# A fp32 encoder trunk on TensorE: another order of products at both ends of each MLP, ScalarE's squares, and smaller first loads

## What is computed

```python
for i in range(DEPTH):                      # 2 layers, x is (1, 512, 1024) float32
    h = rmsnorm(x, norm_mix_g[i])
    x = x + (pool_mixer(h, ...) if i == 0 else sgu_mixer(h, ...))
    h = rmsnorm(x, norm_mem_g[i]); m = rmsnorm(mem, norm_memkv_g[i])   # 256 memory tokens
    x = x + mem_attention(h, m, w_q, w_kv, w_o)                        # 4 heads
    h = rmsnorm(x, norm_ffn_g[i])
    x = x + jnp.square(jax.nn.relu(h @ w1)) @ w2                       # 1024 -> 4096 -> 1024
return rmsnorm(x, final_norm_g)
```

## Time and profile before

| what | value |
|---|---|
| median of 3 runs | 1170.44 us (1170.16 to 1172.05) |
| the profiled execution | 1171.35 us, its span 1169.3 us |
| TensorE (PE) busy | 1140.8 us, 98% of the span |
| VectorE (DVE) | 829.2 us, 71% |
| ScalarE (ACT) | 635.7 us, 54% |
| GpSimd (POOL) | 251.3 us, 21% |
| mean granted TensorE clock | 0.993 of full |
| chain that ended last, by engine | PE 82%, DVE 9%, DMA 3%, ACT 3%, issue 2% |

### The profile page before, as it was taken

The page is one execution under the profiler, slowest core; times in us unless marked ns, Lnnn a source line. Parts: engine busy times, 40 slices in busy tenths (PEclk is TensorE's granted clock), DMA queues, the critical chain, the costliest instruction groups (busy, mean ns, idle before and its releaser), DMA issues.

```text
span 1169.3 us, 16188 instructions
## 1 busy us (share of the span) xinstructions
PE 1140.8 (98%) x6556; PEld 1003.9 (86%) x6556; DVE 829.2 (71%) x933; ACT 635.7 (54%) x773; POOL 251.3 (21%) x211
## 2 busy tenths in 40 slices
PE   8999999999999999999999999999989999999997
PEld 6888888989999999788888888888989999999975
DVE  7787647677786786777487656655757678677778
ACT  7664434765555655545444432543576656556555
POOL 0040035113012121113164044004511211112020
PEclk9999999999999999999999999999999999999999
DMA  9523134969789777735232622313587977977673
GB/s 349 206 80 101 55 135 107 244 133 192 196 181 201 186 143 164 174 73 198 91 97 84 216 91 72 108 36 144 118 227 158 198 191 179 207 171 154 146 133 102
DMA packets 48457, 176.59 MB, mean 151 GB/s; under 512 B 5504, under 2 KB 5632, under 8 KB 47744
## 3 DMA queue, kind: packets, MB, share of 16 engines
q0 software_dynamic: 18432, 67.12, 31.9%
q1 hardware_dynamic: 28368, 104.35, 26.5%
q10 hardware_dynamic: 1584, 4.10, 1.0%
HBM read 173.45 MB, written 2.10 MB: 150 GB/s over the span
## 4 chain that ended last, share of the span: by engine, by line
PE 82%; DVE 9%; DMA 3%; ACT 3%; issue 2%; POOL 0%; SPq 0%; DVEq 0%; ACTq 0%; POOLq 0%
PE psum L1874 11%; PE psum L1876 11%; PE psum L1875 11%; PE psum L2149 8%; PE psum L2150 8%; PE psum L2151 8%; PE psum L2129 8%; PE psum L2131 7%; PE psum L2130 7%; DVE w_lo L1181 2%; DMA w_raw<-in_up 2%; DMA w_raw<-in_weights 1%; DVE w_lo L1170 1%; PE psum L2066 1%; ACT w_hi L725 1%
## 5 line engine op out<-in xcount | busy, mean ns | idle before, releaser
L1181 DVE TENSOR_TENSOR w_lo<-w_sum,w_hi 128x1024 fp32r<-128x1024 f32 x112 | 136.5, 1223 | 84.2 <-ACT w_hi L725 83.9
L2149 PE MATMUL psum<-w_lo,slot_hi 128*128 128x512 f32 x448 | 176.3, 394 | 5.2 <-DVE y_rows L1519 5.2
L2150 PE MATMUL psum<-w_hi,slot_hi 128*128 128x512 f32 x448 | 176.3, 393 | 0.0
L2151 PE MATMUL psum<-w_hi,slot_lo 128*128 128x512 f32 x448 | 175.6, 392 | 0.0
L725 ACT ACTIVATE w_hi<-w_sum 128x1024 fp32r<-128x1024 f32 x112 | 117.7, 1054 | 79.8 <-PE psum L2151 76.0
L2129 PE MATMUL psum<-xs_s_lo,w_hi 128*128 128x256 f32 x512 | 145.4, 284 | 0.9 <-DVE a L1457 0.8
L2131 PE MATMUL psum<-xs_s_hi,w_lo 128*128 128x256 f32 x512 | 144.9, 283 | 0.0
L2130 PE MATMUL psum<-xs_s_hi,w_hi 128*128 128x256 f32 x512 | 144.8, 283 | 0.0
L1827 POOL DMA_DIRECT2D w_sum<-in_down x64 | 55.4, 866 | 373.5 <-DVE w_lo L1181 373.5
L1181 DVE TENSOR_TENSOR w_lo<-w_raw,w_hi 128x1024 fp32r<-128x1024 f32 x80 | 101.0, 1265 | 48.7 <-ACT w_hi L725 48.4
L725 ACT ACTIVATE w_hi<-w_raw 128x1024 fp32r<-128x1024 f32 x80 | 83.9, 1056 | 80.0 <-PE psum L2131 64.1
(11 more groups left out here) (226 smaller groups left out, 2701.1 us busy)
## 6 DMA issues: line engine op xcount, KB each, us to landing
w_raw<-in_weights SPq DMA_DIRECT2D x90, 512.0 KB, 3.7
w_sum<-in_down POOLq DMA_DIRECT2D x64, 512.0 KB, 6.9
w_sum<-in_down SPq DMA_DIRECT2D x48, 512.0 KB, 4.5
w_raw<-in_up POOLq DMA_DIRECT2D x48, 512.0 KB, 6.4
w_raw<-in_up SPq DMA_DIRECT2D x32, 512.0 KB, 3.9
up<-in_up SPq DMA_DIRECT2D x16, 512.0 KB, 4.3
up<-in_up POOLq DMA_DIRECT2D x16, 512.0 KB, 7.2
x<-in_x_t SPq DMA_DIRECT2D x2, 1024.0 KB, 8.8
```

Source lines behind the costliest of these rows:

```text
L1181: dve.tensor_tensor(w_lo[:, c % RING, :], buffer(kind, SUM_BUFFER[STAGE[p][0]] + half), w_hi[:, c % RING, :].bitcast(F32), ALU.subtract).t ...
L2149: pe.matmul(to, s_hi[:, k, tok], w_lo[:, c % RING, cols], start=first, stop=False, skip_group_check=True)
L2150: pe.matmul(to, s_hi[:, k, tok], w_hi[:, c % RING, cols], start=False, stop=False, skip_group_check=True)
L2151: last = pe.matmul(to, s_lo[:, k, tok], w_hi[:, c % RING, cols], start=False, stop=(kp == 1 and j == 1), skip_group_check=True)
```

## The change

1. **End of each MLP.** After block 3's up P3 the order was D P6, U P6, D P7, U P7, D P4, U P4 (D of block 2, U of block 3), then block 3's D. It is now U P6, D P6, U P7, U P4, D P7, D P4. All engines and the order of the weights follow.
2. **Start of each MLP.** `c11` stands ahead of a weight split, `c12` and `c22` are placed in halves between the splits, ScalarE splits weights ahead of `squared`; SP loads quarter "11" of the down weights alone, and the other loads later.
3. **Squares.** ScalarE squares x into two buffers behind the three projections, POOL copies the first and adds seven. `SUMMED` and the buffers' sizes follow.
4. **The kernel's start.** The first memory tile comes first, then chunk 0 in two halves, each split by itself (ScalarE 128x512, VectorE 128x512), and the first chunk's four products run in the order 0, 2, 1, 3. The splits of x stand two to four weight chunks later on ScalarE and VectorE; chunks 10, 11 and the pool weights are split earlier.

```diff
              ("P2", 1), ("P7", 0), ("P7", 1), ("P4", 0), ("P4", 1))
+LAST_UPS = (("D", "P1"), ("U", "P1"), ("D", "P2"), ("U", "P2"), ("D", "P5"), ("U", "P5"), ("D", "P3"), ("U", "P3"),
+            ("U", "P6"), ("D", "P6"), ("U", "P7"), ("U", "P4"), ("D", "P7"), ("D", "P4"))
 READS = ("P1", "P2", "P5", "P3", "P6", "P7", "P4")
...
     steps = [("U", 0, p, h) for p in ORDER for h in range(2)]
-    for b in range(FB - 1):
+    for b in range(FB - 2):
         for p in ORDER:
             steps += [("D", b, p, h) for h in range(2)] + [("U", b + 1, p, h) for h in range(2)]
+    steps += [(kind, FB - 2 + (kind == "U"), p, h) for kind, p in LAST_UPS for h in range(2)]
     return tuple(steps + [("D", FB - 1, p, h) for p, h in LAST_DOWN])
...
-            load(0, 0)
             mem_piece(0)
+            sp.dma_start(w_raw[:, 0, COLS[0]], weights[0, :, COLS[0]]).then_inc(first_loaded, 16)
+            sp.dma_start(w_raw[:, 0, COLS[1]], weights[0, :, COLS[1]]).then_inc(w_loaded[0], 16)
             load(1, 1)
             mem_piece(1)
             mem_piece(2)
             load(2, 2)
+            mem_piece(3)
             load(3, 3)
             next_load(4)
+            next_load(5)
             x_half(0)
-            for c in range(5, 8):
-                next_load(c)
+            next_load(6)
+            next_load(7)
             x_half(1)
...
                         quarter(l, "U", 0, name, half)
+                sp.wait_ge(lo_ready, N.lo[f"xs{l}", "P4"] + 1)
+                for half in range(2):
+                    quarter(l, "D", 0, "11", half)
+                refill(l, "U", 0, "P4")
                 refill(l, "U", 0, "P2")
-                sp.wait_ge(lo_ready, N.lo[f"xs{l}", "P4"] + 1)
-                for name in ("11", "22"):
-                    for half in range(2):
-                        quarter(l, "D", 0, name, half)
+                for half in range(2):
+                    quarter(l, "D", 0, "22", half)
                 refill(l, "U", 0, "P7")
-                refill(l, "U", 0, "P4")
                 for b in range(FB - 1):
...
+            def square_tile(norm, m):
+
+                if m >= 2:
+                    act.wait_ge(ssq_step, KT * norm + m - 1)
+                act.activation(two_squares[:, m % 2, :], x[:, m, :], ACT.Square).then_inc(squares_ready, 1)
+
             def hi_residual_tile(xkey, g, m):
...
                     act.activation(xg[:, m, :], x[:, m, :], ACT.Copy, scale=gain(f"ffn{l}", m)).then_inc(gained_ready, 1)
+                    square_tile(1 + 3 * l, m)
                     if m == 3:
...
                 ahead("U", 0, "P7", 0)
+                ahead("U", 0, "P7", 1)
                 squared(0, 1, a12, "P6")
-                ahead("U", 0, "P7", 1)
+                ahead("U", 0, "P4", 0)
                 operand(0, "P2", a12, h=1)
-                ahead("U", 0, "P4", 0)
+                ahead("U", 0, "P4", 1)
                 squared(0, 2, a22, "P7")
-                ahead("U", 0, "P4", 1)
                 for b in range(FB - 1):
...
                     ahead("U", c, "P3", 1)
+                    if c == FB - 1:
+                        break
                     ahead("D", b, "P6", 0)
...
                     ahead("U", c, "P4", 1)
+                ahead("U", c, "P6", 0)
+                keep_p3(c)
+                ahead("U", c, "P6", 1)
+                ahead("D", b, "P6", 0)
+                ahead("D", b, "P6", 1)
+                squared(c, 1, a12, "P6")
+                ahead("U", c, "P7", 0)
+                operand(c, "P1", a11, h=0)
+                ahead("U", c, "P7", 1)
+                ahead("U", c, "P4", 0)
+                squared(c, 2, a22, "P7")
+                ahead("U", c, "P4", 1)
+                ahead("D", b, "P7", 0)
+                last_quarter(c)
+                ahead("D", b, "P7", 1)
+                ahead("D", b, "P4", 0)
+                operand(c, "P2", a12, h=1)
+                ahead("D", b, "P4", 1)
                 b = FB - 1
-                last_quarter(b)
                 ahead("D", b, "P1", 0)
...
                 x_part("P6", xg[:, 0:4, TOK[0]])
+                c11(0)
                 ahead("U", 0, "P5", 0)
-                c11(0)
                 x_part("P4", xg[:, 4:8, TOK[1]])
                 ahead("U", 0, "P5", 1)
                 ahead("U", 0, "P3", 0)
                 operand(0, "P1", a11)
                 ahead("U", 0, "P3", 1)
                 ahead("U", 0, "P6", 0)
-                ahead("U", 0, "P6", 1)
                 dve.wait_ge(ssq_step, SUMMED[norm])
                 c12(0, half=0)
+                ahead("U", 0, "P6", 1)
+                c12(0, half=1)
                 ahead("U", 0, "P7", 0)
-                c12(0, half=1)
                 row_scales()
+                c22(0, half=0)
                 ahead("U", 0, "P7", 1)
-                c22(0, half=0)
+                c22(0, half=1)
+                ahead("U", 0, "P4", 0)
                 operand(0, "P2", a12)
-                ahead("U", 0, "P4", 0)
-                c22(0, half=1)
                 ahead("U", 0, "P4", 1)
...
                     ahead("U", c, "P3", 1)
+                    if c == FB - 1:
+                        break
                     ahead("D", b, "P6", 0)
...
                     ahead("U", c, "P4", 1)
+                ahead("U", c, "P6", 0)
+                ahead("U", c, "P6", 1)
+                c12(c)
+                ahead("D", b, "P6", 0)
+                ahead("D", b, "P6", 1)
+                ahead("U", c, "P7", 0)
+                read(b, "P6")
+                operand(c, "P1", a11)
+                c22(c, half=0)
+                ahead("U", c, "P7", 1)
+                c22(c, half=1)
+                ahead("U", c, "P4", 0)
+                ahead("U", c, "P4", 1)
+                ahead("D", b, "P7", 0)
+                sum_s1(c)
+                ahead("D", b, "P7", 1)
+                sum_s3(c)
+                sum_s2(c)
+                ahead("D", b, "P4", 0)
+                read(b, "P7")
+                operand(c, "P2", a12)
+                ahead("D", b, "P4", 1)
+                sum_s4(c)
                 b = FB - 1
-                sum_s1(b)
                 ahead("D", b, "P1", 0)
-                sum_s3(b)
                 operand(b, "P5", s1)
+                read(b - 1, "P4")
                 ahead("D", b, "P1", 1)
-                sum_s2(b)
-                sum_s4(b)
+                operand(b, "P3", a12)
                 ahead("D", b, "P2", 0)
-                operand(b, "P3", a12)
                 read(b, "P1")
...
         def _(pool):
-            steps = [0]
-
-            def sum_squares(key, first=0, end=KT):
+            def sum_squares(norm, first=0, end=KT):
 
                 for m in range(first, end):
-                    pool.wait_ge(taken, N.bank[key, m] + 1)
-                    if steps[0]:
-                        pool.wait_ge(ssq_step, steps[0])
-                    dst = ssq if m == 0 else x2
-                    pool.tensor_tensor(dst[:], x[:, m, :], x[:, m, :], ALU.mult).then_inc(ssq_step, 1)
-                    steps[0] += 1
-                    if m:
-                        pool.wait_ge(ssq_step, steps[0])
-                        pool.tensor_tensor(ssq[:], ssq[:], x2[:], ALU.add).then_inc(ssq_step, 1)
-                        steps[0] += 1
+                    pool.wait_ge(squares_ready, KT * norm + m + 1)
+                    if m == 0:
+                        pool.tensor_copy(ssq[:], two_squares[:, 0, :]).then_inc(ssq_step, 1)
+                    else:
+                        pool.wait_ge(ssq_step, KT * norm + m)
+                        pool.tensor_tensor(ssq[:], ssq[:], two_squares[:, m % 2, :], ALU.add).then_inc(ssq_step, 1)
...
                     for p in ("P1", "P5", "P3", "P6"):
+                        if (b, p) == (FB - 2, "P6"):
+                            add_quarters(l, "U", b + 1, p)
+                            add_quarters(l, "D", b, p)
+                            continue
                         add_quarters(l, "D", b, p)
                         if b < FB - 1:
                             add_quarters(l, "U", b + 1, p)
 
-            sum_squares("o0", 0, KT - 1)
+            sum_squares(1, 0, KT - 1)
             add_quarters(0, "U", 0, "P1")
-            sum_squares("o0", KT - 1)
+            sum_squares(1, KT - 1)
             mlp(0)
             for i, m in enumerate(GATE_ORDER):
-                pool.wait_ge(squares_ready, KT + i + 1)
+                pool.wait_ge(squares_ready, 2 * KT + i + 1)
                 if i == 0:
                     pool.tensor_copy(ssq[:], row_sq[:, m, :]).then_inc(ssq_step, 1)
                 else:
-                    pool.wait_ge(ssq_step, steps[0])
+                    pool.wait_ge(ssq_step, 2 * KT + i)
                     pool.tensor_tensor(ssq[:], ssq[:], row_sq[:, m, :], ALU.add).then_inc(ssq_step, 1)
-                steps[0] += 1
             pool.wait_ge(sgu_loaded, 64)
...
                 sums(f"stat_ffn{l}", ST, norm=norm)
```

(36 more changed lines are left out.)

59 lines of the change are left out of this document (38 added, 21 removed).

## The result

| what | before | changed |
|---|---|---|
| median | 1170.44 us (5 runs, 1169.29 to 1172.05) | 1178.26 us (5 runs, 1177.56 to 1182.13) |
| ratio | | 1.0072, 95% interval 1.0053 to 1.0092 |
| profiled execution, its span | 1171.35, 1169.3 us | 1177.56, 1175.6 us |
| mean granted clock | 0.993 | 0.988 |

What follows compares the result with a forecast made beforehand. TensorE, busy 1140.8 of 1169.3 us, was taken as the bound, so only its waits count. Ends +20.6, starts -12.5, opening -2.4 and squares 0 sum to +5.7, giving 1176.1 us, range 1167 to 1182.

Steps and rivals of the forecast that it cites:

- The ends: End of each MLP: two new read waits and slow clock, less the old P5 wait; +20.6 us for both MLPs.
- Wait A: Between D P7 and D P4: TensorE waits 5.9 us for VectorE's read, with the weight load as limit.
- Wait B: Between D P4 and block 3's P1: TensorE waits 5.1 us for VectorE's read of D P4.
- The clock: Behind each of the two new waits per MLP: TensorE at half clock, costing 1.7 us each time.
- The starts: Start of each MLP: waits for c11 and late weights shrink and slow stretches go; -12.5 us over both layers.
- The opening: Kernel's start: memory tile first and half-chunk weight splits bring the first products forward; -2.4 us.
- The squares: Behind the three projections: ScalarE's 24 squares stay hidden; cost 0, with up to 0.8 us gain not excluded.
- rival 1: MLP ends: clock holds and wait A is 4.0, so 1165.5 us; chance 0.22 including a no-change case.
- rival 2: MLP ends: VectorE comes to the reads in time, so ends only gain; 1147 us, chance 0.06.
- rival 3: MLP starts: a raw quarter stays late, each start gives only 4 us; 1181 us, chance 0.18 together with rival 4.
- rival 5: Kernel's start: the opening changes nothing; 1178.5 us, inside the forecast's range, no chance of its own given.
- rival 4: MLP ends: later loads or a longer slow stretch; 1180 to 1183 us, chance 0.18 together with rival 3.

Runs made afterwards that it cites:

- only_ends: The kernel before with only the new order at the end of each MLP; 1192.81 us, ratio to before 1.0192.
- filled: The changed kernel with unused matmuls, 20 in each wait for D P7's read and 18 in each for D P4's; 1169.65 us.
- ob_old_starts: one_between with the old order at the start of each MLP; 1161.94 us, ratio to before 0.9928.
- one_between: The changed kernel with up P4 between D P7 and D P4, and each read right behind its product on VectorE; 1152.42 us.
- ob_old_squares: one_between with GpSimd squaring x as before and ScalarE's squares gone; 1154.56 us, ratio to before 0.9866.
- reads_first: The changed kernel with the reads of D P7 and D P4 moved forward on VectorE alone; 1161.62 us, ratio to before 0.9926.

## Why the prediction was right

The forecast had the sign, the place and the mechanism, and the time within 2.2 us: +5.7 forecast, +7.8 measured, +6.2 between the profiled executions. By its terms:

- *The ends, forecast +20.6.* The traces have +20.9, the runs +22.6 and +22.7. That the traces come so close is in part luck: the four waits were to be 22.0 us and are 20.5, the slow clock behind them was to be 6.8 and is 8.6, and the 0.2 us for `c22`'s half at each up P4 do not appear.
- *Wait A, forecast 5.9; it is 5.26 and 5.53.* (T is the end of up P4.) The working let `s1` start at T + 2.45, but ScalarE splits a later weight half (461.55) ahead of the relu of up P4, and `s1` starts at T + 3.40 (464.75) in both layers. It made the load the limit, with the `w_lo` behind it at T + 5.2. In layer 0 the two paths tie: `s1` ends at 465.98, and `w_hi`, which had waited 0.31 us for its transfer, at 465.99; the `w_lo` starts at T + 4.67. In layer 1 the load is the limit, by 0.33 us, and the `w_lo` starts at T + 4.95:

```profile
1108.70 1.23 DVE L1225 TENSOR_TENSOR w_lo<-w_sum,w_hi 128x1024 fp32r<-128x1024 f32 x1 [0.33 <-ACT w_hi L736]
```

In only_ends the same `w_lo` waits 0.79 us for `w_hi` in layer 0, starts at T + 5.4, and wait A is 6.00, as the working has it (1.01 and 6.22 in layer 1). So the load was rightly in the sum, but only the last 0 to 1.0 us of the wait hang on it; with `s1` alone as the limit the wait is the 5.26 of layer 0. By the Trainium skill's fit (DMA: Bandwidth & Descriptors, Anatomy of one DMA), an estimate of 3.2 us for the load, wait A was to be 4.7; the four loads of `w_sum` issued from SP's queue between 455 and 467 us took 3.6 in the median, and both measured waits (5.26 and 5.53) lie above 4.7.
- *Wait B, forecast 5.1; it is 4.86 twice.* Its parts are 1.13 to the first `w_lo`, 1.14 and 1.14, and 1.45 for the read and the signal, where 1.29, 1.14, 1.13 and 1.55 were forecast.
- *The clock, inside that term, forecast 1.7 for each of four waits, 6.8.* This was the term of the ends that was too small: behind the four waits the products lose 8.6 us by the trace, and 8.6 by the run filled. The stretches in the earlier trace rows, some 3.4 us, came behind waits of 2.0 to 2.7 us; behind one of 4.9 us it was 5.1.
- *The starts, forecast -12.5.* The trace has 6.0 + 6.7 = 12.7 between up P1 and the first down product. That holds part of the squares' gain, and the starts alone are worth 9.5 in ob_old_starts. Of the 3.2 us between the two readings 1.7 are a slow stretch which that run did not have; that the rest is the squares fits their size and is not shown by a run of its own.
- *The opening, forecast -2.4.* -1.9 in the traces of the two kernels, -2.8 in the runs.
- *The squares, forecast 0.* This step failed in size: they gain 2.1 us. The cover that I named holds: ScalarE's 24 squares of 0.62 us show in no wait of TensorE. But I had put the benefit for VectorE in the bound (0.8) and not in the sum. In one_between the two `w_lo` ahead of `xs_a_lo` take 2.35 us together and `xs_a_lo` 2.02, in ob_old_squares 3.20 and 2.31, and with that the waits for x's low part are back. I had also read the 2.32 of the earlier trace rows as beside a square of GpSimd's; the square (193.98 to 195.93 us) ran beside the two `w_lo`, and `xs_a_lo` beside the add that follows it. The rule of the Trainium skill (GPSIMD Engine Reference, 1. Specifications), that VectorE's instructions with two SBUF inputs contend with GpSimd, pointed the right way, and these durations agree with it; the size is the runs' 2.1.
- *The rivals.* That the clock might hold (rival 1) was refuted for waits of 5 us by the rows of the changed kernel, and is half true for waits near 2 us. That the read might not be in the way (rival 2) would have needed another order on VectorE or on TensorE; reads_first and one_between show what such orders are worth, 16.6 and 25.8 us. Poor starts (rival 3) and an idle opening (rival 5) did not come. The longer slow stretch of rival 4 came in part: 8.6 us in place of 6.8, not 13.6.
- *The arithmetic.* Three figures of the prediction are a little off by its own terms: with a load that never limits wait A comes to 4.3 and not 4.7 (3.67 + 4 x 1.14 + 1.40 + 0.15 - 5.45), with the fit's 3.2 us to 4.6, and the bounds by the load to 1172.3 and 1180.3 and not to 1172.8 and 1180.5. None of them changes the forecast.

Why the new order was worse, in a sentence: it took the up products out from between D P7, D P4 and block 3's D P1, which share a pair of banks, and so laid bare two reads of VectorE, behind two to five instructions whose results TensorE did not need yet.

## What to carry to other kernels

Before two products that use the same banks one after the other are put side by side, write down what stands ahead of the first one's read on the reading engine, and add it up from the end of the first product; that sum, not the read's own 1.4 us, is the wait. If the products must stay side by side, the read goes first in that engine's order, or the second product gets other banks, and then the next consumer in line has to be looked at in the same way. Count the slow clock behind a wait as part of its price: here it was 8.6 us beside waits of 20.5.
